# Two products of a Strassen slab change places: B22 ahead of T2, and VectorE's reads are reordered with them

## What is computed

```python
def sq_relu_mlp(h, w_up, w_down):
    return jnp.square(jax.nn.relu(h @ w_up)) @ w_down

gate, up = jnp.split(h2 @ w_ffn_in[l], 2, axis=-1)
x = x + (jax.nn.silu(gate) * up) @ w_ffn_out[l]
```

## Time and profile before

| | |
|---|---|
| median of 3 runs | 1810.84 us (1810.82 to 1811.19) |
| the profiled execution | 1811.19 us, span 1809.5 us |
| TensorE busy | 1794.8 us, 99% of the span |
| VectorE busy | 1270.9 us, 70% |
| ScalarE busy | 808.7 us, 45% |
| GpSimd busy | 288.0 us, 16% |
| granted TensorE clock | 0.999 |

### The profile page before, as it was taken

The page is one execution under the profiler, slowest core; times in us unless marked ns, Lnnn a source line. Parts: engine busy times, 40 slices in busy tenths (PEclk is TensorE's granted clock), DMA queues, the critical chain, the costliest instruction groups (busy, mean ns, idle before and its releaser), DMA issues.

```text
span 1809.5 us, 21889 instructions
## 1 busy us (share of the span) xinstructions
PE 1794.8 (99%) x8580; PEld 1455.8 (80%) x8580; DVE 1270.9 (70%) x1680; ACT 808.7 (45%) x1064; POOL 288.0 (16%) x237
## 2 busy tenths in 40 slices
PE   9999999999999999999999999999999999999998
PEld 7888888888877668888888878788887888888886
DVE  7896858686879865767686887666446455846757
ACT  6753534343534863444343454566323343323334
POOL 0004000000145864000000031111001321011012
PEclk9999999999999999999999999999999999999999
DMA  6233253443234003452524222122332223431612
GB/s 234 94 117 116 71 186 90 127 133 94 65 99 148 16 2 116 139 163 47 186 56 154 65 85 84 56 70 71 98 112 82 94 93 140 140 117 47 175 59 76
DMA packets 152053, 186.25 MB, mean 103 GB/s; under 512 B 7472, under 2 KB 120240, under 8 KB 151952
## 3 DMA queue, kind: packets, MB, share of 16 engines
q1 hardware_dynamic: 143712, 165.93, 28.1%
q0 software_dynamic: 7696, 18.41, 4.9%
q10 hardware_dynamic: 544, 0.52, 0.1%
HBM read 182.58 MB, written 2.14 MB: 102 GB/s over the span
## 4 chain that ended last, share of the span: by engine, by line
PE 87%; DVE 8%; ACT 2%; issue 1%; POOL 1%; DMA 0%; SPq 0%; DVEq 0%; ACTq 0%; POOLq 0%
PE bank L998 27%; PE bank L1000 26%; PE bank L999 26%; PE bank L1034 1%; PE bank L1219 1%; DVE work L2460 1%; PE bank L1245 1%; DVE t L2457 1%; DVE wlo L2058 1%; DVE XC L2155 1%; PE bank L1354 1%; PE bank L1372 1%; ACT whi L1481 1%; DVE sq_e L2566 1%; PE bank L1223 1%
## 5 line engine op out<-in xcount | busy, mean ns | idle before, releaser
L998 PE MATMUL bank<-Ahi,whi 128*128 128x512 f32 x1400 | 550.2, 393 | 1.4 <-DVE wlo L2084 1.1
L1000 PE MATMUL bank<-Ahi,wlo 128*128 128x512 f32 x1400 | 545.1, 389 | 0.0
L999 PE MATMUL bank<-Alo,whi 128*128 128x512 f32 x1400 | 544.9, 389 | 0.0
L2058 DVE TENSOR_TENSOR wlo<-stage,whi 128x2048 fp32r<-128x2048 f32 (+1 forms) x133 | 304.8, 2292 | 175.2 <-ACT whi L1481 175.1
L1481 ACT ACTIVATE whi<-stage 128x2048 fp32r<-128x2048 f32 (+1 forms) x139 | 262.7, 1890 | 218.8 <-PE bank L1000 192.6
L998 PEld LDWEIGHTS bank<-Ahi,whi 128*128 128x128 f32 x1400 | 262.2, 187 | 64.7 <-issue 7.9
L1000 PEld LDWEIGHTS bank<-Ahi,wlo 128*128 128x128 f32 x1400 | 262.2, 187 | 55.9
L999 PEld LDWEIGHTS bank<-Alo,whi 128*128 128x128 f32 x1400 | 262.3, 187 | 55.5 <-issue 1.2
L998 PE MATMUL bank<-whi,Hh 128*128 128x512 f32 x602 | 234.8, 390 | 0.0
L999 PE MATMUL bank<-wlo,Hh 128*128 128x512 f32 x602 | 234.3, 389 | 0.0
L1000 PE MATMUL bank<-whi,Hl 128*128 128x512 f32 x602 | 234.2, 389 | 0.0
(11 more groups left out here) (356 smaller groups left out, 2468.1 us busy)
## 6 DMA issues: line engine op xcount, KB each, us to landing
stage<-in_mlp_w_up SPq DMA_DIRECT2D x32, 1024.0 KB, 5.4
stage<-in_w_in SPq DMA_DIRECT2D x22, 1024.0 KB, 5.1
stage<-in_w_ffn_in SPq DMA_DIRECT2D x22, 1024.0 KB, 4.9
quad<-in_mlp_w_down SPq DMA_DIRECT2D x16, 1024.0 KB, 6.8
stage<-in_mlp_w_down SPq DMA_DIRECT2D x16, 1024.0 KB, 4.8
quad<-in_mlp_w_down POOLq DMA_DIRECT2D x8, 1024.0 KB, 8.6
stage<-in_rec_w_in SPq DMA_DIRECT2D x6, 1024.0 KB, 5.3
stage<-in_att_w_in SPq DMA_DIRECT2D x6, 1024.0 KB, 5.1
```

Source lines behind the costliest of these rows:

```text
L998: e.matmul(ps, hi, rh, start=first, stop=False, skip_group_check=onto)
L999: e.matmul(ps, hi, rl, start=False, stop=False, skip_group_check=onto)
L1000: return e.matmul(ps, lo, rh, start=False, stop=last, skip_group_check=onto)
L2058: e.tensor_tensor(lo_of(u)[:, 0:nk, 0:n], source(u), f32(hi_of(u)[:, 0:nk, 0:n]), ALU.subtract).then_inc(s_lo[slot_of[u]], 1)
```

## The change

The order of the products becomes B11, B21, T1, B22, T2, T3, T4. `LEFT`, `BANK`, `MIDDLE` and `follows` are changed to match: bank p holds B11, then T2, T3 and T4 on it, bank r T1 and then B22. ScalarE's reads in a fresh slab free the ring's bank after B22. Units, weight slots and staging follow `RIGHT`, so ScalarE's and VectorE's split of B22 comes ahead of that of T2. In VectorE's order the read of T1's first bank moves in front of T2's low part; the second bank's read and the difference T4 follow it.

```diff
-RIGHT = ["B11", "B21", "T1", "T2", "B22", "T3", "T4"]
-LEFT = [0, 1, 4, 5, 6, 3, 2]
-BANK = ["p", "q", "r", "p", "r", "p", "p"]
+RIGHT = ["B11", "B21", "T1", "B22", "T2", "T3", "T4"]
+LEFT = [0, 1, 4, 6, 5, 3, 2]
+BANK = ["p", "q", "r", "r", "p", "p", "p"]
...
-    MIDDLE = {0: 0, 2: 1, 3: 2, 5: 3}
+    MIDDLE = {0: 0, 2: 1, 4: 2, 5: 3}
...
-            follows = {3: 0, 4: 2, 5: 3, 6: 5}
+            follows = {3: 2, 4: 0, 5: 4, 6: 5}
...
-                    e.activation(sum_of(t + j, h), ring.bank((*key, BANK[r], j))[:, :], ACT.Copy, scale=float(SIGN[r])).then_inc(s_mid_read, 1)
+                    e.activation(sum_of(t + j, h), ring.bank((*key, BANK[r], j))[:, :], ACT.Copy, scale=float(SIGN[r])).then_inc(*((s_mid_read, 1) if r in MIDDLE else ring.take((*key, BANK[r], j))))
...
             add_sum(key, 0, 0, fresh)
             add_sum(key, 0, 1, fresh)
-            for r in range(1, 5):
+            lo(u + 3)
+            add_sum(key, 1, 0, fresh)
+            add_sum(key, 1, 1, fresh)
+            add_sum(key, 2, 0, fresh)
+            lo(u + 4)
+            add_sum(key, 2, 1, fresh)
+            difference(key, "T4")
+            for r in (3, 4):
                 lo(u + r + 2)
                 add_sum(key, r, 0, fresh)
                 add_sum(key, r, 1, fresh)
-                if r == 2:
-                    difference(key, "T4")
             if after:
                 lo(u + 7)
```

## The result

The changed kernel took 1816.74 us (median of 8 runs, 1815.46 to 1817.36), the kernel before, run beside it, 1811.01 (8 runs, 1810.31 to 1812.64): a ratio of 1.003, 95% interval 1.0021 to 1.0039. It is slower, as forecast, but the median lies 1.8 us above the 1814.9 of the forecast and 0.7 us above its range. The profiled execution took 1816.71 us with a span of 1815.0; that of before had 1811.19 and 1809.5.

What follows compares the result with a forecast made beforehand. TensorE was taken as the bound, busy 1794.8 of 1809.5 us, so new waits add in full: 0.56 (fresh slabs) + 1.14 (fd 0) + 2.32 (fd 2) = 4.0 us on a median of 1810.84 gives 1814.9 us; range 1813.7 to 1816.0.

Steps and rivals of the forecast that it cites:

- fd 0: First FFN slab: TensorE waits for VectorE's reads ahead of B22 and T3; cost 1.14 us.
- fd 2: Last FFN slab, 18 matmuls per product: TensorE stops about 1.5 us at B22 and again at T3; cost 2.32 us.
- the row of additions: VectorE's operations in a slab added up from difference T2, giving 1561.95 in fd 0 for T1's first bank read.
- the fresh slabs: First slab of each of two MLPs: T3 waits for VectorE's read of the fifth product; 0.28 us each, 0.56 both.
- the steady slabs: Slabs g = 1 to 3 of both MLPs, six in all: reads come in time, 0.34 us to spare ahead of T3; cost 0.
- the third rival: Steady slabs and fd 1 stop too ahead of T3, 0.2 us in each of seven: 1816.3 us; chance 0.12.
- the first rival: VectorE's vanished pauses pay for the change, 0.2 us back in fd 0 and fd 2: 1810.4 us; chance 0.06.
- The price of a resumption: After a late bank read, TensorE resumes as if its first matmul started 0.20 us after the release; bounds 0 and 0.34.
- The second rival: TensorE loads weights while waiting and resumes at once, four times 0.20 us less: 1814.1 us; chance 0.12.
- The closing norm follows T3's and T4's sums in the queues of VectorE, ScalarE, GpSimd and SP and moves by the same time.: Behind fd 2: the norm shifts with T3's and T4's sums, adding nothing to that slab's 2.32 us.
- On the median: 1814.9 us: Whole kernel: the 4.0 us sum added to the earlier median of 1810.84 us; chance 0.70.
- If a stop of 1.5 us costs something afterwards: Sign against the forecast: after TensorE's stop, for instance in fd 2, a lower granted clock would add time; no size given.

Runs made afterwards that it cites:

- Experiments 1 and 2: New order of products in the MLP slabs alone (1812.76 us, ratio 1.0006), then in the FFN slabs alone (1815.93 us, ratio 1.0025), each against the kernel before.
- experiment 4: Changed kernel's product order, with VectorE reading T1's and T2's banks earlier in fd 0, fd 2 and the fresh slabs: 1813.84 us, ratio 1.0012 to the kernel before.
- experiment 5: Changed kernel with GpSimd's six closing-norm multiplications cut from 512 columns to 32: one run, 1816.07 us.
- The second comparison: Changed kernel run again without edit, beside the kernel before: 1816.64 us against 1812.00, ratio 1.0024.
- Experiment 3: Changed kernel's product order with VectorE's old sequence, T1's first bank read after T2's low part: 1828.67 us, ratio 1.0096 to the kernel before.

## Why the prediction was wrong, and where it was right

**The mechanism and the slabs** came as forecast. B22 waits for the read of T1's first bank, in fd 0 and fd 2, and T3 for the read of the product ahead of it. In fd 0 and fd 2 VectorE's queue alone sets the time of each, and its starts, counted from the difference T2, came within 0.06 us of the row of additions; in the fresh slabs VectorE stands 3.14 us ahead of T4's low part, waiting for ScalarE's high part, as forecast. Experiments 1 and 2 put the costs in the two places, and experiment 4 takes them away by moving the reads. Nothing stops in the steady slabs: the third rival falls. In dn 0 1 the read ahead of T3 is finished at 317.17 and T3 starts at 317.51, so a read with 0.34 us to spare suffices, as one with 0.29 does in fd 1. The time that this rival gave, 1816.3, lies near the measured one by coincidence. The pauses that VectorE lost didn't bring T1's read forward beyond what was worked out: the first rival falls.

**The price of a resumption** was a little small: 0.22 us behind the release in fd 0 and fd 2, 0.24 in the fresh slabs (0.32 where 0.28 was forecast), not 0.20. With some hundredths elsewhere the slabs cost 0.12 us more than forecast. The second rival falls: in fd 0 the load starts 0.11 us behind the release and not during the wait. By the Trainium skill (TensorE: Matmul & The Clock Gate, "Step-by-step: what each phase is for") loads are pulled ahead of running matmuls. That section says nothing of a queue stopped at a wait, and rival 2 stretched it to one: in fd 0 no matmul ran during the wait, and the load came only behind the release.

**The first step that failed** is "The closing norm follows T3's and T4's sums in the queues of VectorE, ScalarE, GpSimd and SP and moves by the same time." It moved by 0.34 us more. Not all of the norm was shifted alike: GpSimd's last multiplications moved by 4.7 us from profile to profile (1800.88 to 1805.56 for the fifth), VectorE's first scaling by 5.2 (1801.84 to 1807.02). So the scaling met the sixth multiplication just begun, and not the fifth near its end (experiment 5). With the price this makes the change's own cost 4.5 us and not 4.0: 1815.3 us, which the range still held.

**The step that put the measurement outside** is "On the median: 1814.9 us". The sum was added to a median of three runs, 1810.82 to 1811.19, which all lie in the lower of the two groups. In the 72 runs of the kernel before that this study has, 43 lie at 1810.17 to 1811.64 (median 1810.92) and 29 at 1811.96 to 1812.85 (median 1812.36). In the 18 of the changed kernel it is 7 at 1814.81 to 1816.24 (median 1815.58) and 11 at 1816.61 to 1817.36 (median 1816.71). One run of each kernel, 1811.64 and 1816.24, lies between the groups; counted to the upper ones they change no median by more than 0.1. Group against group the change costs 4.7 and 4.4 us. The result's 5.7 is this, and the difference between the groups where one median fell into the lower and one into the upper. The second comparison, with both medians in the upper group, gave 1816.64 - 1812.00 = 4.6. That the changed kernel falls into the upper group more often (11 of 18 against 29 of 72) these runs can't settle: in the first comparison it is 6 of 8 against 2 of 8, in the second 5 of 9 against 10 of 18. So the mechanism and most of the sum were right, and that the median fell outside the range was in part the draw.

**The range** had no term for this. Its bounds took in the price alone; the profile before showed one execution of the lower group, and three runs that agree within 0.4 us were taken for its spread.

**"If a stop of 1.5 us costs something afterwards"** doesn't apply: the pitch behind the stop in fd 2 was 0.23 us. Experiment 3 shows the limit from the other side: at 3.1 us it costs 1.6 us more.

## What to carry to other kernels

Where a consumer's bank comes free by one engine's queue, add up that queue operation by operation: it gave the cost of each slab here within 0.05 us, and it shows which read to move ahead. When a chain is shifted, follow its last stage too, against engines that aren't shifted by the same time; a moved step can run beside another one and cost twice as much. And before a small sum is added to a median of few runs, ask in which group of executions that median lies; compare groups with groups.

## What the runs showed of the hardware that was not expected

- VectorE's scaling of 128x512 took 0.48 us alone, 0.62, 1.36 and (experiment 4) 1.57 with GpSimd's multiplication beside it, and ended 0.28 or 0.29 us behind that.
- TensorE's granted clock stayed at 1.00 after standing still for 1.0 and 1.5 us, and fell to 0.51 for 3.5 us after 3.1 us (experiment 3, fd 2), beginning some 0.8 us after the matmuls had resumed. After 3.2 us (fd 0) it fell while TensorE still stood: it was 0.67 from 1569.50 to 1570.00, and the matmuls resumed at 1570.18.
- Near 1085 us, behind the same small matmuls, it fell to 0.50 in one execution and not in another of the same kernel; at the start the pitch was 0.43 us in two profiles of fourteen, although the record of the granted clock says 1.00 there.
